# State-space pairs at other blocks, GELU and GLU three blocks on, half blocks of projection weights, and another order at the last gate

## The chip, the cores and the metric

One core of a Trainium2 chip (trn2) runs one program. The metric is the device time of one execution in microseconds (us), median of several runs. Five engines work side by side and meet only at semaphores: TensorE (PE, matmuls), VectorE (DVE), ScalarE (ACT), GpSimd (POOL) and SyncE (SP), which here issues the DMAs. Each engine works off its own list strictly in order.

## The reference

Two layers on x of shape (1, 256, 1024), all in float32. Cut to what matters here:

```python
def hybrid_layer(x, ...):
    h = x + 0.5 * swiglu(rms_norm(x, ffn1_norm), ffn1_w_in, ffn1_w_out)
    proj = rms_norm(h, mix_norm) @ w_in
    (sb_qkv, s5_u, gq, gk, gv, gr, gg, dsa_qkv, gates) = split(proj)
    y_sb = stick_breaking_attention(sb_q, sb_k, sb_v)
    y_s5 = s5_mixer(s5_u, ...)       # 1024 complex states, scan over time,
                                     # gelu(y) @ w_glu, then ga * sigmoid(gb)
    y_gla = gla_mixer(gq, gk, gv, gr, gg, ...)
    y_dsa = dilated_mixer(d_q, d_k, d_v, ...)
    gate = sigmoid(gates.reshape(bsz, seq, 4, 1024))
    per_branch = einsum('bsnw,nwd->bsnd', stack(y_sb, y_s5, y_gla, y_dsa), w_branch)
    h = h + sum(gate * per_branch, axis=2) @ w_out
    return h + 0.5 * swiglu(rms_norm(h, ffn2_norm), ffn2_w_in, ffn2_w_out)
```

## The kernel before

All weights come as one stream of blocks of 128 x 2048 floats (1 MB), into a ring of three slots (`raw`). SyncE issues the load of a slot when its last low part is written. A float32 weight is used as two fp32r parts: ScalarE rounds each half of a block (`round_half`, L802, L812) to `w_hi`, VectorE subtracts (`half_rest`, L1068, L1072) to get `w_lo`, and TensorE makes three matmuls of each product (L456 to L458): hi x hi, hi x lo, lo x hi. The activations are split in the same way (`split_pair`; L824 and L1084). So each block costs TensorE 48 matmuls of 256 columns, ScalarE two instructions and VectorE two.

A layer is: ffn 0 (33 blocks), mixer (31 blocks of `SEQ`, then 5 blocks of the output projection in `OUT_TILES`), ffn 1 (33 blocks). The change is in the mixer alone. For each block m, TensorE runs the block's product into bank 0 or 1 and then `pieces(m)` (L662), the small matmuls of the four branches; ScalarE rounds the block three ahead and then does its own `pieces(m)` (L948); VectorE evacuates bank m (L1478), makes the low part of the block three ahead, and does its `pieces(m)` (L1310). The order of each engine is thus written out by hand. Eleven of the blocks 0 to 12 are projections for the branches (`s5u` at 0 to `gr` at 12, dilated v at 11, linear v at 9); gates (q, n) fill blocks 7, 10, 13 to 23, 25, 27 and 29; `out0` to `out3` (blocks 24, 26, 28, 30) multiply the four branch outputs with w_branch.

State-space branch (S5), in four pairs of state tiles: `s5_in(pair)` on TensorE at block S5_AT[pair] into banks 6 and 7, `s5_rotate(pair)` (VectorE, L1252, waits for GpSimd's state of the pair before), one block later `s5_scan(pair)` (L1269, L1274), then GpSimd `s5_pair(pair)` (L1621, L1628 to L1634 and L1536), and four blocks after the rotation `s5_out(pair)` on TensorE (L600). After the last pair come the GELU (VectorE L1391 to L1402 at block 15, tanh on ScalarE, VectorE L1407 at 16), the GLU (TensorE at block 17, L707), tanh of the gate (ScalarE L1006), the product (VectorE L1417 at 18), and the split of the branch output (ScalarE L929, VectorE L1280).

Dilated attention: rotary product on VectorE at blocks 13 and 14 (ends with L1385), transposes by TensorE at 15 (L698), scores at 16 and 17, softmax and exponentials (L1286 to L1289, L997, L998) there, `dilated_weights` (L1292, L1295 to L1301) at 18 and 19, `dsa_turn` (L651, L658) at 19 and 20, the product with v at 21. Gated linear attention uses ScalarE at 16 for a logarithm and an exponential (L1002, L1003).

Banks 4 to 7 are shared: `gla_scores` (block 12) needs them after the last rotation.

After an out block, VectorE multiplies with the gates (`gate(dt)`, L1441, L1452), GpSimd adds the branches (`mix(dt)`, L1636), ScalarE and VectorE split the sum (`mixed_hi`, L1021 and L1025; `mixed_lo`, L1457 and L1459), and TensorE uses it in the output projection (`out_part`, L764). Two of the five projection blocks hold one tile of 128 columns only; their second half is zero and used by no matmul. After each, VectorE adds to h (L1509) and h is split for ffn 1.

Of the kernel before, what the change touches and what calls it, by code (L numbers as in the profile page):

```python
# [8 lines left out]
F32 = mybir.dt.float32  # L9
# [57 lines left out]
S5_AT = (1, 4, 7, 10)  # L67

LAST_OF_U = (3, 3)
MIXED_AT = [((0,), (1,)), ((), ()), ((), ()), ((2, 3, 4, 5, 6), (7,))]  # L70
# [155 lines left out]
def build(nc, x_in, stream, params_in, const_in, out):  # L226
    ctx = ExitStack()
    with ctx:
# [221 lines left out]
        def _(pe):  # L450
# [20 lines left out]
            for layer in range(LAYERS):  # L471
# [97 lines left out]
                def mixer():  # L569
# [16 lines left out]
                    def s5_in(pair):  # L586

                        if pair == 0:
                            pe.wait_ge(s.evac_v, layer * PER.evac_v + NTH[SLOT["s5u"]])
                        else:  # L590
                            pe.wait_ge(s.s5_rot, layer * PER.s5_rot + pair)
                        for part in range(2):
# [34 lines left out]
                    def gla_scores():  # L627
# [3 lines left out]
                        pe.wait_ge(s.s5_rot, layer * PER.s5_rot + ST // 2)  # L631
# [30 lines left out]
                    def pieces(m):  # L662
# [27 lines left out]
                        if m == 15:  # L690
# [3 lines left out]
                            pe.wait_ge(s.dsa_rope, layer * PER.dsa_rope + 1)  # L694
                            for side in range(2):
# [9 lines left out]
                        if m == 17:  # L705
                            dsa_scores(2), dsa_scores(3)
                            pe.wait_ge(s.s5_gelu, layer * PER.s5_gelu + 1)  # L707
# [7 lines left out]
                        if m == 19:  # L715
                            dsa_turn(0), dsa_turn(1)
                        if m == 20:
                            dsa_turn(2), dsa_turn(3)
# [71 lines left out]

        def ffn_steps(f):
# [9 lines left out]
        def _(act):  # L801
            def round_half(layer, k, slot, half):  # L802
# [6 lines left out]
                elif first_block(layer, k, slot):  # L809
# [3 lines left out]
                    .then_inc(s.w_hi, 1)  # L813

            def round_weights(layer, k, slot):

                round_half(layer, k, slot, 0)
                round_half(layer, k, slot, 1)
# [25 lines left out]
            for layer in range(LAYERS):  # L844
# [103 lines left out]
                def pieces(m):  # L948
# [39 lines left out]
                    if m == 15:  # L988
# [3 lines left out]
                        act.wait_ge(s.s5_inner, layer * PER.s5_inner + 1)  # L992
                        act.activation(s5g[:, 1, :], s5g[:, 1, :], ACT.Tanh).then_inc(s.s5_tanh, 1)
# [10 lines left out]
                    if m == 17:  # L1004
                        act.wait_ge(s.s5_glu, layer * PER.s5_glu + 1)
                        act.activation(s5g[:, 1, :], banks[:, 5, :], ACT.Tanh, scale=0.25).then_inc(s.s5_sig, 1)  # L1006
                    if m == 18:
                        act.wait_ge(s.y, layer * PER.y + 1)
                        branch_hi(1, yb[:, 0, :, :].rearrange("p a t -> p (a t)"), 0.25)
                    if m in (19, 20):  # L1010
                        for h in (2 * m - 38, 2 * m - 37):
                            act.wait_ge(s.dsa_pt, layer * PER.dsa_pt + h + 1)
                            act.activation(attB[:, h, :], banks[:, 6 + h % 2, 0:ATT], ACT.Copy) \
                                .then_inc(s.dsa_pte, 1)
                    if m == 21:
                        act.wait_ge(s.y, layer * PER.y + 2)
                        branch_hi(2, yb[:, 1, :, :].rearrange("p a t -> p (a t)"), 0.5)
# [772 lines left out]
```

## Time and profile before

| | |
|---|---|
| median of 3 runs | 1288.61 us (1288.47 to 1292.49) |
| profiled execution | 1289.22 us, its span 1287.3 us |
| granted TensorE clock, mean | 0.992 |
| TensorE busy | 1245.8 us (97%) |
| VectorE busy | 895.5 us (70%) |
| ScalarE busy | 640.0 us (50%) |
| GpSimd busy | 327.4 us (25%) |
| mixer of layer 0, layer 1 | about 209 to 455 us, 844 to 1090 us |

The span runs from the first to the last instruction of the profiled execution. The busy time of TensorE is an upper bound of its work, since matmuls overlap; the gap between two starts is the measure. A wait is put down to the engine whose semaphore came last; "issue" is time in which nothing that the profile shows was waited for, and the program's order then says what it was.

### The profile page before, as it was taken

Reading aid. Unit: us, or ns where it says so; the run is one execution under the profiler, and the core shown is the slowest. Engines: PE = TensorE matmul, PEld = TensorE weight load, DVE = VectorE, ACT = ScalarE, POOL = GpSimd, SP = SyncE. Lnnn points to the kernel's source line nnn. Section 1 sums busy time; section 2 is a strip of 40 time slices with the busy share of each in tenths; the row PEclk is TensorE's granted clock in tenths of the full one; section 3 lists DMA queues with packets and bytes.
Section 4 is the critical chain, followed back from the end, with each engine's and each line's share of the span. In section 5 each row is a group of like instructions: output and inputs, shape, how many; then the busy total and the mean of one; then the engine's idle time right before and its main releaser. Section 6 shows DMA issues by size and latency. Waiting matters only on the chain.

```text
span 1287.3 us, 25597 instructions
## 1 busy us (share of the span) xinstructions
PE 1245.8 (97%) x10328; PEld 1222.4 (95%) x10328; DVE 895.5 (70%) x1172; ACT 640.0 (50%) x904; POOL 327.4 (25%) x462
## 2 busy tenths in 40 slices
PE   5999999999999999999999999999999999999998
PEld 5999999888999999999999999998889999999998
DVE  4766857877877676555676687687887786656554
ACT  5654545663544454444456445557625444534432
POOL 0388800364003300000005895005630041000000
PEclk9999999998999999999999999999999999999999
DMA  7555554542344365555545545544333454555541
GB/s 299 199 185 174 180 179 165 175 149 99 131 158 166 135 236 198 191 195 168 191 135 201 188 165 200 189 164 152 135 130 131 154 186 160 201 184 175 186 173 66
DMA packets 31029, 220.46 MB, mean 171 GB/s; under 512 B 3568, under 2 KB 3568, under 8 KB 4592
## 3 DMA queue, kind: packets, MB, share of 16 engines
q1 hardware_dynamic: 30960, 219.49, 49.0%
q8 instruction: 50, 0.82, 0.3%
q14 instruction: 19, 0.16, 0.0%
HBM read 218.42 MB, written 1.05 MB: 170 GB/s over the span
## 4 chain that ended last, share of the span: by engine, by line
PE 75%; DVE 12%; POOL 7%; ACT 3%; issue 2%; DMA 0%; DVEq 0%; SPq 0%; ACTq 0%
PE banks L456 24%; PE banks L457 24%; PE banks L458 24%; DVE w_lo_t L1072 5%; PE banks L469 3%; ACT w_hi_t L812 1%; POOL st L1631 1%; DVE s5x L1274 1%; POOL s5x L1629 1%; POOL s5x L1628 1%; POOL st L1634 1%; POOL st L1536 1%; POOL st L1632 1%; DVE u_lo_t L1084 1%; DVE hT L1223 1%
## 5 line engine op out<-in xcount | busy, mean ns | idle before, releaser
L1072 DVE TENSOR_TENSOR w_lo_t<-raw,w_hi_t 128x1024 fp32r<-128x1024 f32 x408 | 518.0, 1310 | 107.8 <-ACT w_hi_t L812 107.4
L812 ACT ACTIVATE w_hi_t<-raw 128x1024 fp32r<-128x1024 f32 x408 | 407.2, 1046 | 126.7 <-PE banks L458 126.0
L456 PE MATMUL banks<-u_hi_t,w_hi_t 128*128 128x256 f32 x1520 | 436.0, 287 | 18.2 <-DVE w_lo_t L1072 14.1
L457 PE MATMUL banks<-u_lo_t,w_hi_t 128*128 128x256 f32 x1520 | 431.9, 284 | 0.0
L458 PE MATMUL banks<-u_hi_t,w_lo_t 128*128 128x256 f32 x1520 | 431.9, 284 | 0.0
L456 PEld LDWEIGHTS banks<-u_hi_t,w_hi_t 128*128 128x128 f32 x1520 | 293.6, 193 | 22.5 <-DVE w_lo_t L1072 14.1
L457 PEld LDWEIGHTS banks<-u_lo_t,w_hi_t 128*128 128x128 f32 x1520 | 293.8, 193 | 0.1
L458 PEld LDWEIGHTS banks<-u_hi_t,w_lo_t 128*128 128x128 f32 x1520 | 293.5, 193 | 0.0
L456 PE MATMUL banks<-b_hi_t,w_hi_t 128*128 128x256 f32 x864 | 245.1, 284 | 1.9 <-DVE b_lo_t L1084 1.9
L457 PE MATMUL banks<-b_lo_t,w_hi_t 128*128 128x256 f32 x864 | 244.5, 283 | 0.0
L458 PE MATMUL banks<-b_hi_t,w_lo_t 128*128 128x256 f32 x864 | 244.5, 283 | 0.0
L456 PE MATMUL banks<-h_hi_t,w_hi_t 128*128 128x256 f32 x672 | 190.9, 284 | 2.2 <-DVE h_lo_t L1177 1.2
L457 PE MATMUL banks<-h_lo_t,w_hi_t 128*128 128x256 f32 x672 | 190.4, 283 | 0.0
L458 PE MATMUL banks<-h_hi_t,w_lo_t 128*128 128x256 f32 x672 | 190.4, 283 | 0.0
L849 ACT ACTIVATE sbqk<-sbqk 128x256 f32<-128x256 f32 x88 | 36.8, 418 | 266.5 <-DVE sbqk L1167 266.5
L456 PEld LDWEIGHTS banks<-b_hi_t,w_hi_t 128*128 128x128 f32 x864 | 165.8, 192 | 2.3 <-DVE b_lo_t L1084 2.3
L457 PEld LDWEIGHTS banks<-b_lo_t,w_hi_t 128*128 128x128 f32 x864 | 165.8, 192 | 0.0
L458 PEld LDWEIGHTS banks<-b_hi_t,w_lo_t 128*128 128x128 f32 x864 | 165.8, 192 | 0.0
L456 PEld LDWEIGHTS banks<-h_hi_t,w_hi_t 128*128 128x128 f32 x672 | 129.3, 192 | 2.8 <-issue 1.3
L457 PEld LDWEIGHTS banks<-h_lo_t,w_hi_t 128*128 128x128 f32 x672 | 129.2, 192 | 0.0
L458 PEld LDWEIGHTS banks<-h_hi_t,w_lo_t 128*128 128x128 f32 x672 | 129.2, 192 | 0.0
L1167 DVE TENSOR_TENSOR sbqk<-banks,rstd_row 128x512 f32<-128x512 f32 x88 | 60.6, 689 | 74.5 <-PE banks L458 74.2
(215 smaller groups left out, 1267.7 us busy)
## 6 DMA issues: line engine op xcount, KB each, us to landing
raw<-weights SPq DMA_DIRECT2D x203, 1024.0 KB, 4.9
prm<-params SPq DMA_DIRECT2D x1, 1178.5 KB, 5.3
prm<-params SPq DMA_DIRECT2D x1, 1166.5 KB, 15.1
cst<-constants SPq DMA_DIRECT2D x1, 1027.0 KB, 11.1
hT<-x_t SPq DMA_DIRECT2D x2, 512.0 KB, 5.5
raw<-weights SPq DMA_DIRECT2D x2, 512.0 KB, 6.4
out_t<-hT SPq DMA_DIRECT2D x4, 256.0 KB, 2.2
prm<-params SPq DMA_DIRECT2D x1, 12.0 KB, 1.9
```

The costliest lines, as they stand in the source:

```text
L456: pe.matmul(o, st[0], mv[0], start=start, stop=False, skip_group_check=True)
L457: pe.matmul(o, st[0], mv[1], start=False, stop=False, skip_group_check=True)
L458: ins = pe.matmul(o, st[1], mv[0], start=False, stop=stop, skip_group_check=True)
L469: return pe.matmul(o, st, mv, start=start, stop=stop, skip_group_check=True)
L812: act.activation(w_hi[:, slot, a:a + HALF], raw[:, slot, a:a + HALF], ACT.Copy) \
L849: act.activation(ab[:, buf, 0, :], ab[:, buf, 0, :], ACT.Silu).then_inc(s.h_silu, 1)
L1072: dve.tensor_tensor(w_lo[:, slot, a:a + HALF], raw[:, slot, a:a + HALF], w_hi[:, slot, a:a + HALF].bitcast(F32), ALU.subtract).then_inc(s. ...
L1084: ins = dve.scalar_tensor_tensor(out=in_lo[where][:, kt, :], in0=hT[:, kt, :], scalar=p_(name)[:, kt:kt + 1], in1=in_hi[where][:, kt, :].b ...
L1167: dve.tensor_tensor(ab[:, buf, :, :], banks[:, bank, :].rearrange("p (c t) -> p c t", c=2), rstd_row[:, :].unsqueeze(1).to_broadcast([P, 2 ...
L1223: dve.scalar_tensor_tensor(out=hT[:, 2 * q:2 * q + 2, :].rearrange("p a t -> p (a t)"), in0=banks[:, q, :], scalar=0.5, in1=hT[:, 2 * q:2 ...
L1274: ins = dve.tensor_tensor_scan(s5x[:, i % 2, 1, part, :], decay, s5x[:, i % 2, 0, part, :], 0.0, ALU.mult, ALU.add)
L1536: own.link(pool.tensor_tensor(o, a, b, op))
```

## The change

Three edits, all in the mixer. (1) `S5_AT` becomes 1, 5, 9, 13, so the rotations, scans and outputs of pairs 1 to 3 move. `gla_scores` then stands before pair 3's product: it waits for three rotations instead of four, `s5_in(3)` waits for the masks of the linear attention, and the transposes at block 15 wait for the fourth rotation. The GELU moves from blocks 15 and 16 to 18 and 19, the GLU from 17 to 20, the gate's tanh to 20 and the product to 21, so that branch 2's split comes before branch 1's. (2) A one-tile block is rounded and subtracted in its first half only, and the semaphores count two for it; the splits of h for ffn 1 come after the weights. (3) At `out3`, VectorE does gate 6 before the four low parts, and gate 7 before the weights; ScalarE does `mixed_hi(6)` after the weights.

```diff
--- before.py
+++ after.py
...
 SS_AFTER, ROW_AFTER = 3, 5
-S5_AT = (1, 4, 7, 10)
+S5_AT = (1, 5, 9, 13)
 
 LAST_OF_U = (3, 3)
-MIXED_AT = [((0,), (1,)), ((), ()), ((), ()), ((2, 3, 4, 5, 6), (7,))]
+MIXED_AT = [((0,), (1,)), ((), ()), ((), ()), ((2, 3, 4, 5), (6, 7))]
 
...
                             pe.wait_ge(s.s5_rot, layer * PER.s5_rot + pair)
+                        if pair == 3:
+                            pe.wait_ge(s.gla_attm, layer * PER.gla_attm + HEADS)
                         for part in range(2):
...
                         pe.wait_ge(s.sb_exp, layer * PER.sb_exp + HEADS)
-                        pe.wait_ge(s.s5_rot, layer * PER.s5_rot + ST // 2)
+                        pe.wait_ge(s.s5_rot, layer * PER.s5_rot + 3)
                         for i in range(NGC):
...
                             pe.wait_ge(s.dsa_rope, layer * PER.dsa_rope + 1)
+                            pe.wait_ge(s.s5_rot, layer * PER.s5_rot + ST // 2)
                             for side in range(2):
...
                             dsa_scores(2), dsa_scores(3)
+                        if m == 19:
+                            dsa_turn(0), dsa_turn(1)
+                        if m == 20:
+                            dsa_turn(2), dsa_turn(3)
                             pe.wait_ge(s.s5_gelu, layer * PER.s5_gelu + 1)
...
                             ins.then_inc(s.s5_glu, 1)
-                        if m == 19:
-                            dsa_turn(0), dsa_turn(1)
-                        if m == 20:
-                            dsa_turn(2), dsa_turn(3)
                         if m == 21:
...
 
+        def one_tile(k, slot):
+
+            o = k * RING + slot - FFN_BLOCKS - NSEQ if isinstance(k, int) else -1
+            return 0 <= o < len(OUT_TILES) and len(OUT_TILES[o]) == 1
+
         def ffn_steps(f):
...
                 act.activation(w_hi[:, slot, a:a + HALF], raw[:, slot, a:a + HALF], ACT.Copy) \
-                    .then_inc(s.w_hi, 1)
+                    .then_inc(s.w_hi, 2 if one_tile(k, slot) else 1)
 
...
                 round_half(layer, k, slot, 0)
-                round_half(layer, k, slot, 1)
+                if not one_tile(k, slot):
+                    round_half(layer, k, slot, 1)
 
...
                         act.activation(dkT, banks[:, 7, :], ACT.Copy).then_inc(s.dsa_qk, 1)
-                        act.wait_ge(s.s5_inner, layer * PER.s5_inner + 1)
-                        act.activation(s5g[:, 1, :], s5g[:, 1, :], ACT.Tanh).then_inc(s.s5_tanh, 1)
                     if m in (16, 17):
...
                         act.activation(gn[:, 3, :], gn[:, 3, :], ACT.Exp, scale=-0.5).then_inc(s.gla_y0, 1)
-                    if m == 17:
-                        act.wait_ge(s.s5_glu, layer * PER.s5_glu + 1)
-                        act.activation(s5g[:, 1, :], banks[:, 5, :], ACT.Tanh, scale=0.25).then_inc(s.s5_sig, 1)
                     if m == 18:
-                        act.wait_ge(s.y, layer * PER.y + 1)
-                        branch_hi(1, yb[:, 0, :, :].rearrange("p a t -> p (a t)"), 0.25)
+                        act.wait_ge(s.s5_inner, layer * PER.s5_inner + 1)
+                        act.activation(s5g[:, 1, :], s5g[:, 1, :], ACT.Tanh).then_inc(s.s5_tanh, 1)
                     if m in (19, 20):
...
                                 .then_inc(s.dsa_pte, 1)
+                    if m == 20:
+                        act.wait_ge(s.s5_glu, layer * PER.s5_glu + 1)
+                        act.activation(s5g[:, 1, :], banks[:, 5, :], ACT.Tanh, scale=0.25).then_inc(s.s5_sig, 1)
                     if m == 21:
+                        act.wait_ge(s.y, layer * PER.y + 1)
+                        branch_hi(2, yb[:, 1, :, :].rearrange("p a t -> p (a t)"), 0.5)
                         act.wait_ge(s.y, layer * PER.y + 2)
-                        branch_hi(2, yb[:, 1, :, :].rearrange("p a t -> p (a t)"), 0.5)
+                        branch_hi(1, yb[:, 0, :, :].rearrange("p a t -> p (a t)"), 0.25)
                         act.wait_ge(s.dsa_o, layer * PER.dsa_o + 1)
...
                 dve.tensor_tensor(w_lo[:, slot, a:a + HALF], raw[:, slot, a:a + HALF],
-                                  w_hi[:, slot, a:a + HALF].bitcast(F32), ALU.subtract).then_inc(s.w_lo, 1)
+                                  w_hi[:, slot, a:a + HALF].bitcast(F32), ALU.subtract) \
+                    .then_inc(s.w_lo, 2 if one_tile(k, slot) else 1)
 
...
                 half_rest(layer, k, slot, 0)
-                half_rest(layer, k, slot, 1)
+                if not one_tile(k, slot):
+                    half_rest(layer, k, slot, 1)
 
...
 
+                    if m in (16, 17):
+                        dilated_softmax(2 * m - 32), dilated_softmax(2 * m - 31)
+                    if m == 16:
+                        dve.wait_ge(s.gla_tanh, layer * PER.gla_tanh + 1)
+                        own.link(dve.scalar_tensor_tensor(out=gn[:, 2, :], in0=gn[:, 2, :], scalar=1.0,
+                                                          in1=gr[:, :, :].rearrange("p a t -> p (a t)"),
+                                                          op0=ALU.add, op1=ALU.mult))
+                    if m == 18:
                         dve.wait_ge(s.s5_y, layer * PER.s5_y + ST // 2)
...
                             .then_inc(s.s5_inner, 1)
-                    if m in (16, 17):
-                        dilated_softmax(2 * m - 32), dilated_softmax(2 * m - 31)
-                    if m == 16:
+                    if m == 19:
                         dve.wait_ge(s.s5_tanh, layer * PER.s5_tanh + 1)
...
                                                  op0=ALU.add, op1=ALU.mult).then_inc(s.s5_gelu, 1)
-                        dve.wait_ge(s.gla_tanh, layer * PER.gla_tanh + 1)
-                        own.link(dve.scalar_tensor_tensor(out=gn[:, 2, :], in0=gn[:, 2, :], scalar=1.0,
-                                                          in1=gr[:, :, :].rearrange("p a t -> p (a t)"),
-                                                          op0=ALU.add, op1=ALU.mult))
                     if m in (18, 19):
                         dilated_weights(2 * m - 36), dilated_weights(2 * m - 35)
-                    if m == 18:
+                    if m == 21:
                         dve.wait_ge(s.s5_sig, layer * PER.s5_sig + 1)
...
                                                  op0=ALU.add, op1=ALU.mult).then_inc(s.y, 1)
-                    if m == 19:
-                        branch_lo(1, 1, yb[:, 0, :, :].rearrange("p a t -> p (a t)"), 0.25)
                     if m == 20:
...
                     if m == 22:
-                        branch_lo(2, 2, yb[:, 1, :, :].rearrange("p a t -> p (a t)"), 0.5)
+                        branch_lo(2, 1, yb[:, 1, :, :].rearrange("p a t -> p (a t)"), 0.5)
+                        branch_lo(1, 2, yb[:, 0, :, :].rearrange("p a t -> p (a t)"), 0.25)
                         branch_lo(3, 3, banks[:, 3, :], 1.0)
...
                             q = int(SEQ[m][3])
+                            gate(2 * q)
                             if q == 3:
...
                                     mixed_lo(dt)
-                            gate(2 * q)
+                                gate(2 * q + 1)
                             rest_of_weights(layer, k0 + m // RING + 1, m % RING)
-                            gate(2 * q + 1)
+                            if q < 3:
+                                gate(2 * q + 1)
                             continue
...
                             dve.wait_ge(s.res, layer * PER.res + 8 + q + 1)
-                        if o < 2:
-                            split_pair(layer * 3 + 2, "g_ffn2", q, where=1)
                         if o < 4:
                             rest_of_weights(layer, k0 + m // RING + 1, m % RING)
-                        if o in (2, 4):
+                        if o != 3:
                             split_pair(layer * 3 + 2, "g_ffn2", q, where=1)
```

## Rows read from the trace of the kernel before

**Rows 1.** The page, its first part: busy time of TensorE.

```profile
PE 1245.8 (97%) x10328; PEld 1222.4 (95%) x10328; DVE 895.5 (70%) x1172; ACT 640.0 (50%) x904; POOL 327.4 (25%) x462
```

**Rows 2.** Waits of TensorE over the whole span: us in total, times, longest.

```profile
PE banks L456 <- DVE w_lo_t L1072: 15.0, 2, 14.1
PE banks L469 <- POOL st L1634: 7.8, 6, 2.4
PE banks L469 <- issue: 5.6, 7, 2.2
PE banks L456 <- DVE u_lo_t L1459: 3.8, 2, 1.9
...
PE banks L456 <- DVE b_lo_t L1084: 1.9, 2, 1.0
```

**Rows 3.** Windows behind gaps: length, busy PE, PEld, DVE, ACT, POOL, clock, DMA.

```profile
248.50:260.50 12.00, 12.00 (x100) 11.39 (x101) 11.86 (x17) 5.68 (x10) 1.78 (x1) 1.00 0.26 90
...
884.10:898.10 14.00, 14.00 (x104) 13.37 (x104) 13.72 (x18) 6.19 (x12) 3.78 (x3) 0.88 0.21 76
304.20:319.20 15.00, 14.95 (x162) 14.33 (x163) 7.81 (x11) 0.60 (x1) 10.44 (x12) 0.66 0.42 141
939.60:951.50 11.90, 11.81 (x161) 11.07 (x162) 7.84 (x11) 0.60 (x1) 9.25 (x11) 0.86 0.50 178
...
1075.40:1087.60 12.20, 12.20 (x89) 12.20 (x90) 7.88 (x11) 8.66 (x12) 0.00 (x0) 0.86 0.25 88
```

**Rows 4.** Timeline of VectorE, blocks 4 to 11: start, duration, idle before it.

```profile
248.48 1.23 DVE L1262 TENSOR_TENSOR s5x<-banks,G 128x1024 f32<-128x1024 f32 x1 [4.40 <-POOL st L1634]
...
297.26 1.22 DVE L1262 TENSOR_TENSOR s5x<-banks,G 128x1024 f32<-128x1024 f32 x1
...
300.86 2.35 DVE L1072 TENSOR_TENSOR w_lo_t<-raw,w_hi_t 128x1024 fp32r<-128x1024 f32 x2
303.13 1.02 DVE L1322 SCALAR_TENSOR_TENSOR attA<-attA,cst 128x384 f32<-128x384 f32 x2
```

**Rows 5.** Timeline of GpSimd, its first, second and last step of pair 2.

```profile
281.69 0.74 POOL L1628 TENSOR_TENSOR s5x<-s5x,G 128x256 f32<-128x256 f32 x1 [9.42 <-DVE s5x L1274]
282.39 1.72 POOL L1629 TENSOR_TENSOR s5x<-s5x,G 128x256 f32<-128x256 f32 x1
...
293.41 1.59 POOL L1634 TENSOR_TENSOR st<-s5x,st 128x256 f32<-128x256 f32 x1
```

**Rows 6.** Timeline of VectorE from the end of block 13 to block 18.

```profile
319.27 0.69 DVE L1478 SCALAR_TENSOR_TENSOR G<-banks,rstd_row 128x512 f32<-128x512 f32 x1 [5.48 <-PE banks L458]
...
332.39 1.23 DVE L1385 TENSOR_TENSOR dqk<-dqk,G 128x1024 f32<-128x1024 f32 x1
...
337.49 0.86 DVE L1393 SCALAR_TENSOR_TENSOR s5x<-s5u,prm,banks 128x256 f32<-128x256 f32 x2
...
339.58 0.69 DVE L1401 TENSOR_TENSOR s5x<-s5x 128x512 f32<-128x512 f32 x1
...
352.50 2.36 DVE L1072 TENSOR_TENSOR w_lo_t<-raw,w_hi_t 128x1024 fp32r<-128x1024 f32 x2 [3.78 <-ACT w_hi_t L812]
...
361.80 0.29 DVE L1295 CUSTOM_DVE_ANT_0 attB<-attB,cst 128x128 f32<-128x128 f32 x1
```

**Rows 7.** Timeline of TensorE at blocks 15, 17, 18 and 19.

```profile
334.12 1.03 PE L698 MATMUL banks<-cst,dqk 128*128 128x128 f32 x8
...
348.50 3.72 PE L469 MATMUL banks<-s5x,prm 128*128 128x256 f32 x16
351.87 0.47 PE L456 MATMUL banks<-u_hi_t,w_hi_t 128*128 128x256 f32 x1
...
363.56 0.49 PE L658 MATMUL banks<-cst,attB 128*128 128x128 f32 x3
364.62 0.55 PE L658 MATMUL banks<-cst,attB 128*128 128x128 f32 x3 [0.57 <-DVE attB L1301]
```

**Rows 8.** Timeline of ScalarE at out3: the high part of tile 6.

```profile
434.89 0.42 ACT L1025 ACTIVATE u_hi_t<-U 128x256 fp32r<-128x256 f32 x1 [5.07 <-POOL U L1641]
```

## The prediction

> **What bounds the kernel now.** The page comes first: TensorE is busy for 97% of the span, so a change can only win TensorE's idle time or its slow clock, and can only lose by adding either [rows 1]. The waits of TensorE come second, since they say where the idle time is. One wait of 14.1 us is the start and is not touched. The rest is small and lies in the mixer of both layers: 7.8 us on GpSimd's state (L1634, six waits of s5_out), "issue" with 2.2 us in each layer (the first attention at block 12), 0.57 us on the dilated weights of block 19 and about as much at block 20 (L1301 [rows 7]), and at the end of the mixer 3.8 us on L1459, 1.9 us on L1084 and 0.9 us on L1072 [rows 2]. Third, the windows behind such gaps, for the granted clock. Seven gaps of 1.9 to 2.4 us stand in the mixers. Behind four the clock was partly 1.2 instead of 2.4 GHz: (1 - 0.88) x 14.0 = 1.7 us lost, (1 - 0.66) x 15.0 = 5.1 behind block 12 of layer 0, where the same work took 15.0 us against 11.9 in layer 1, 1.7 there, and 1.7 near the end; behind the other three, as at 248.5, it stayed at 2.4 [rows 3]. Last, the timelines of VectorE and GpSimd: the reader is to see there that VectorE's queue stands still before a rotation (4.40 us), and is late for the attention afterwards (L1322 starts at 303.13, and TensorE waits for it) [rows 4].
>
> I count in blocks m as the program does, 5.8 us each: two of them take from 351.87 to 363.56 [rows 7].
>
> **Part 1, early half (blocks 1 to 12).** Pair 1 to 3 move from blocks 4, 7, 10 to 5, 9, 13, and their outputs from 8, 11, 14 to 9, 13, 17. Pair 0 stays, and so does its wait at block 5 (2.0 us); s5_in(1) now fills time in front of it, and s5_rotate(1) no longer finds an unfinished state: the 4.40 us of idle VectorE go [rows 4]. Layer 0, in times of the old trace: rotation 1 now ends near 255.6, its scan near 264.0, behind block 6's weights and the softplus pieces. GpSimd needs 13.3 us for a pair (281.69 to 295.0); its steps take 0.74 alone and 1.7 beside L1072 [rows 5]. State 1 is there at 277.2. TensorE reaches s5_out(1) at 276.9 (block 9's end at 275.7, then s5_in(2)): a wait of 0.3 instead of 2.4. Then VectorE is what counts up to the attention. ScalarE ends its softplus part at 275.7, has rounded half of block 9 at 277.6, and from there VectorE has weights 2.3, masks 2.1, sum 1.4, rotation 3.6 (297.26 to 300.86 [rows 4]), evacuation 0.6, weights 2.3, gate products 2.9, scan 2.4, weights 2.9 beside GpSimd, L1322 1.0: 299.1. TensorE is ready at 297.6. So the attention starts 5.1 us earlier, but 2.1 us of that is work only put off (s5_in(3), s5_out(2)): a gain of **3.0 us**. In layer 1 the gap at block 5 was followed by the slow clock, and the wait at block 8 was 0.7, not 2.4: the slow clock hid in the wait. The gain is **1.4 us**. Bounds: 1.5 and 0.5 if GpSimd and VectorE block each other for one or two steps more; 4.6 and 2.9 if every wait behind block 5 goes. I take the middle, by the rows' durations.
>
> **Part 1, late half (blocks 13 to 23).** Here the moved work lands on VectorE in front of what TensorE needs. I count from the end of block 13, which is 319.2 in the old trace [rows 6].
> - Block 15: the transposes (L698) need the rotary product L1385, which ends at 333.5, +14.4, with TensorE there at +14.9 (334.12 [rows 7]). Rotation 3 (3.6 us) now stands before it in block 13: +18.0. TensorE has s5_in(3) and s5_out(2) more and the old s5_out(3) less: +16.1. A new wait of **2.0 us**. The added wait for s5_rot is met long before.
> - Block 17: scan 3 ends at +20.4, and GpSimd needs 12.7 to 13.5 us beside two blocks of weights (8.8 if nothing blocks it): +33.2 to +33.9. TensorE is at s5_out(3) at +31.7. A wait of 2 us, which the next step would contain anyway.
> - Block 19: the head weights of the dilated attention. The chain is block 16's end (+24.9), weights, softmax of heads 0 and 1 (+31.3), ScalarE's exponentials and the two table loads (4.7), weights of block 17 from +37.0 (old row: VectorE idle 3.78 for ScalarE), softmax of heads 2 and 3 (+41.6), weights of block 18 (+43.5 to +45.8). Now the GELU, 2.8 us (337.49 to 340.27), stands before the head weights, 2.7 us (361.80 to 364.5) [rows 6]: +51.2. In the old order the GLU's 3.4 us on TensorE (348.50 to 351.87) were the cover for this chain: its wait was only 0.57 [rows 7]. The GLU is now at block 20, so TensorE finishes block 19 at +47.1 and waits 4 us. Block 20 starts at +51.6; in the old order it started at +45.7 with the GLU done. Without GLU and with the two moved pieces it should have been +44.5: lost **7.1 us**, the 2.0 of block 15 among them.
> - Block 20: the wait on L1301 there goes with its restart, since VectorE is ahead by then: 0.9 back. The GLU costs the same 3.4 there. Block 21 to out0: s5's output, three L1280 instead of two behind block 22's weights end at +79.7, out0 is reached at +80.2. Nothing lost, with 0.5 us to spare.
> Together **+6.1 us** per layer. Bounds: 4 (if the weights find ScalarE earlier) and 9 (if GpSimd lengthens the weights of blocks 15 and 16 and the 0.5 us of spare is used up).
>
> **Part 2 and 3, the end of the mixer.** Old: ScalarE waits 5.07 us for GpSimd's mix before it rounds out3's successor [rows 8], VectorE's weights come after that, then gate 7, then mix 7, and TensorE waits 1.9. Now gate 6 starts at 430.1, gate 7 ends at 433.8, mix 7 on GpSimd at 437.8 at worst, and its low part is there at 438.7, for a need at 440.9. The four L1459 pushed behind gate 6 end from 431.7 to 432.7, one after the other, and TensorE first needs one at 433.0. The halved blocks take 2 x 1.0 us from ScalarE and 2 x 1.2 us from VectorE per layer, and the splits go behind the weights. Block 34 is then ready 5 us early, and the last split ends at 458.1 for a need at 459.0. All of these waits should go: 3.8 + 1.9 + 0.9 = 6.6 us, with restarts of 0.1 to 0.3 us each and 0.3 at the sum of squares 7.6, and 1.5 us of slow clock in layer 1 (of the 1.7, the part in which TensorE has work) [rows 2, 3]: **-9.1 us** for both layers (4.5 + 4.6). Bounds: -9.5 and -6, where the last split comes late by its margin of 0.9 and the slow clock comes anyway. The DMA queue only profits: it waits for the same counter, which now jumps by two.
>
> **The clock.** The new waits at blocks 15 and 19 come in both layers. Four of seven gaps were followed by 1.2 GHz [rows 3], at about 1.6 us: 4 x 0.57 x 1.6 = **+3.6 us**, from 0 to 6.4. The slow clock behind block 17's wait would be hidden in block 19's. The Trainium skill (TensorE: Matmul & The Clock Gate, "Why this matters for your kernels") has the throughput drop only after idle gaps longer than those here; by that these 3.6 us would be nothing. This trace does not agree: gaps of about 2 us were followed by the drop.
>
> **The sum.** -3.0 - 1.4 + 6.1 + 6.1 - 9.1 = -1.3 us, and with the clock +2.3 us. The profiled execution took 1289.2 (span 1287.3 and 1.9 around it), the median is 1288.6, 0.6 lower: 1291.5 for a profile, 1290.9 for the median.
>
> **Rivals.**
> A, no difference to be measured (within 0.3%, 3.9 us, which is about what this kernel's measurement can tell from none): the mid-mixer loses what the end wins. My forecast, 1290.9, alone 1286 to 1293. Chance 0.47.
> B, slower: the dilated chain at block 19 is the one mechanism. For it speaks that everything from block 16 on is one chain through VectorE and ScalarE without slack. It decides from 7.5 us per layer on, or from the slow clock behind all four waits: +2.8 + 2.8 on top of the sum: 1293 to 1298, about 1295.5. Chance 0.34.
> C, faster: the 4.40 us that VectorE no longer idles are carried to block 13, or ScalarE lets the weights of blocks 17 and 18 through earlier, so that block 19 waits 2 us less, and the clock holds: -1.3 - 4 = -5.3 and less, about 1283. Against it: VectorE already has 5.48 us idle before 319.27, so a lead ends there [rows 6]. By the skill's rule on the clock alone the sum would be 1287.3, still A. Chance 0.17.
> D, the end does not do what it says (the low parts stay late, as gate 7 and the weights collide with GpSimd): 9.1 becomes 4: 1296, which is B's side. Chance 0.02.
>
> Faster 0.17, same 0.47, slower 0.36. The range goes from 1284.0, into C, to 1298.0, the end of B.
>
> **What would show it.** Right: waits of TensorE on L1634 at block 8 gone, a wait before L698 of 2 us, a wait before L658 at block 19 of 3 to 5 us with the GELU rows directly before the L1295 rows, and L1459 gone from the waits. Wrong: L658 waits below 2 us, or the attention at block 12 waiting over 3 us.

## The result, and the profile after

The changed kernel takes 1282.8 us (median of 6 runs, 1282.3 to 1286.0) against 1288.6; the ratio is 0.995, with a 95% interval of 0.9935 to 0.9966. It is 0.5% faster. The forecast was 1290.9 with a range down to 1284.0: wrong in sign and 1.2 us outside. The profiled execution has a span of 1281.1 us, 6.2 less than before.

The page of the changed kernel, first part [rows 1]:

```profile
PE 1243.2 (97%) x10328; PEld 1220.3 (95%) x10328; DVE 899.9 (70%) x1168; ACT 636.3 (50%) x900; POOL 335.7 (26%) x462
```

Its waits of TensorE over the span (total, times, longest), to be read beside [rows 2]:

```profile
PE banks L456 <- DVE w_lo_t L1081: 14.3, 1, 14.3
PE banks L469 <- POOL st L1646: 8.6, 6, 2.0
PE banks L660 <- DVE attB L1312: 6.2, 4, 2.7
PE banks L701 <- DVE dqk L1396: 3.4, 2, 1.7
PE banks L456 <- DVE h_lo_t L1188: 1.2, 1, 1.2
PE banks L469 <- issue: 0.6, 3, 0.2
```

Before, the head weights had this line, which [rows 2] leaves out:

```profile
PE banks L658 <- DVE attB L1301: 2.5, 4, 0.7
```

The reader is to see that the waits of the mixer's end are gone (L1459, L1084 and the second of L1072; 6.6 us), that "issue" fell by 5.0, that a new wait stands before the transposes at block 15 (3.4), and that the one for the head weights at block 19 grew (6.2 instead of 2.5). In all the waits fell by little, from 38.0 to 34.5 us. The sum by stretch, both layers together (from the timelines; 2.05 us of work per layer is only put off from the first stretch to the third):

| stretch | forecast | measured |
|---|---|---|
| s5_out(0) to the attention at block 12 | -5.1 - 3.4 | -6.5 - 6.4 |
| from there to the end of block 13 | 0 | -3.2 - 0.1 |
| end of block 13 to out0 | +8.15 + 8.15 + 3.6 (clock) | +11.2 + 9.2 |
| out0 to the sum of squares for ffn 1 | -9.1 | -5.2 - 5.2 |
| sum | +2.3 | -6.2 |

The timeline of TensorE (start, duration, idle before it): s5_out(0), s5_out(1), the transposes, s5_out(3), and the two turns of block 19. The attention of block 12, at 298.24, has no wait.

```profile
248.94 1.06 PE L469 MATMUL banks<-st,s5c 128*32 128x256 f32 x8 [1.36 <-POOL st L1646]
...
278.04 1.06 PE L469 MATMUL banks<-st,s5c 128*32 128x256 f32 x8 [0.95 <-POOL st L1646]
...
298.24 1.57 PE L469 MATMUL banks<-attA,sbv 128*64 128x256 f32 x16
...
328.08 1.09 PE L701 MATMUL banks<-cst,dqk 128*128 128x128 f32 x8 [1.70 <-DVE dqk L1396]
...
343.69 1.06 PE L469 MATMUL banks<-st,s5c 128*32 128x256 f32 x8 [1.96 <-POOL st L1646]
...
360.05 0.55 PE L660 MATMUL banks<-cst,attB 128*128 128x128 f32 x3 [2.74 <-DVE attB L1312]
361.39 0.90 PE L660 MATMUL banks<-cst,attB 128*128 128x128 f32 x3 [0.79 <-DVE attB L1312]
```

VectorE in front of block 19, from the weights of block 18's turn to the head weights; the four lines L1412 to L1420 are the GELU, 355.88 to 358.65:

```profile
353.60 2.36 DVE L1081 TENSOR_TENSOR w_lo_t<-raw,w_hi_t 128x1024 fp32r<-128x1024 f32 x2 [1.22 <-ACT w_hi_t L820]
355.88 0.87 DVE L1412 SCALAR_TENSOR_TENSOR s5x<-s5u,prm,banks 128x256 f32<-128x256 f32 x2
...
357.96 0.69 DVE L1420 TENSOR_TENSOR s5x<-s5x 128x512 f32<-128x512 f32 x1
358.57 0.28 DVE L1306 CUSTOM_DVE_ANT_0 attB<-attB,cst 128x128 f32<-128x128 f32 x1
...
360.98 0.35 DVE L1312 TENSOR_SCALAR attB<-attB,dmx 128x256 f32<-128x256 f32 x1
```

Windows behind waits (length, busy PE, PEld, DVE, ACT, POOL, clock, DMA), beside [rows 3]: 12 us from the attention of block 12 in layer 0 and in layer 1, and block 20 of layer 0.

```profile
298.20:310.20 12.00, 12.00 (x163) 11.45 (x164) 6.00 (x8) 2.52 (x4) 10.08 (x12) 0.86 0.49 176
929.60:941.60 12.00, 12.00 (x163) 11.47 (x164) 6.03 (x8) 2.56 (x4) 10.06 (x12) 0.86 0.51 176
...
361.90:370.10 8.20, 8.20 (x50) 8.20 (x49) 5.44 (x18) 1.39 (x3) 0.00 (x0) 0.66 0.38 130
```

### The profile page after: what moved, and what is told of

Same layout as the page of the kernel before. It is cut to its first block, busy times and chain, and to the rows that moved or that the text cites. A ratio compares the mean times of both kernels' runs of the same rounds, so it can differ in the third digit from the quotient of the medians.

```text
span 1281.1 us, 25591 instructions
## 1 busy us (share of the span) xinstructions
PE 1243.2 (97%) x10328; PEld 1220.3 (95%) x10328; DVE 899.9 (70%) x1168; ACT 636.3 (50%) x900; POOL 335.7 (26%) x462
## 4 chain that ended last, share of the span: by engine, by line
PE 84%; DVE 8%; POOL 5%; ACT 2%; issue 1%; DMA 0%; SPq 0%; DVEq 0%; ACTq 0%
PE banks L456 27%; PE banks L458 27%; PE banks L457 27%; PE banks L469 3%; DVE w_lo_t L1081 3%; POOL st L1643 1%; POOL s5x L1641 1%; DVE s5x L1285 1%; ACT w_hi_t L820 1%; POOL st L1646 1%; POOL s5x L1640 1%; POOL st L1644 1%; DVE u_lo_t L1095 1%; POOL st L1548 1%; DVE hT L1234 1%
## 6 DMA issues: line engine op xcount, KB each, us to landing
cst<-constants SPq DMA_DIRECT2D x1, 1027.0 KB, 11.2
```

## The experiments

All are timed in three rounds against the kernel before on the same chip (its median there 1289.6 to 1290.0). My theory once the result was known: the end wins about 10 us; the late half loses what was forecast; the forecast was wrong about the early half, where it had counted on a wait at block 12 and left the slow clock behind it as it was, and neither came so. The rival: the late half cost less than forecast, and the end did not bring what it should.

### The end alone, and the pairs alone

The first kernel has parts 2 and 3 of the diff, with the pairs, GELU and GLU of before (against the changed kernel, cut to its first lines):

```diff
-S5_AT = (1, 5, 9, 13)
+S5_AT = (1, 4, 7, 10)
...
```

> The kernel before with parts 2 and 3 only (half blocks for the one-tile projection blocks, splits behind the weights, gates 6 and 7 ahead of the weights at out3). Theory: the whole gain of the change comes from here. From out0 to the sum of squares the kernel before takes 74.4 us in each layer and the changed one 69.1; so this kernel is 10.5 us faster than before (about 1278), and L1459, L1084 and L1072 are gone from TensorE's waits but for the start. Rival: the late low parts are late because of the order in blocks 13 to 23; then a part of the 5.2 us per layer stays and the gain is 7 us or less.

Measured: 1276.9 us (1275.1 to 1277.1), ratio 0.990 (0.988 to 0.991): 12.8 faster. Its waits of TensorE:

```profile
PE banks L469 <- POOL st L1642: 7.5, 5, 2.4
PE banks L469 <- issue: 4.3, 5, 2.2
PE banks L658 <- DVE attB L1309: 2.5, 4, 0.7
```

The second has part 1 alone:

> The changed kernel with parts 2 and 3 undone: only the pairs, the GELU and the GLU are moved. Theory: this part alone loses. Early half -6.5 and -6.4 us up to the attention of block 12 (2.1 of each only put off), -3.1 less slow clock behind it, late half +11.2 and +9.2: together +4.3, about 1293; waits before L698, s5_out(3) and the dilated turns as in the changed kernel. Rival: the move wins by itself (removed GpSimd waits), then it is below 1287.

Measured: 1294.8 us (1292.3 to 1297.3), ratio 1.004 (1.002 to 1.006): 5.2 slower. Its waits hold both new ones at the sizes of the changed kernel, and those of the end are back. The late half cost no less than forecast: from the attention of block 14 to the sum of squares it took 9.2 and 9.8 us more than before, 19.0 together, where the forecast's terms for this part make 17.8. With the end's gain that puts the rival out. Its waits:

```profile
PE banks L660 <- DVE attB L1310: 6.2, 4, 2.8
PE banks L456 <- DVE u_lo_t L1469: 3.7, 2, 1.9
PE banks L701 <- DVE dqk L1394: 3.4, 2, 1.7
```

So the pairs lose and the end wins, as forecast, but by +5.2 instead of +11.4 (-3.0 - 1.4 + 12.2 + 3.6), and by -12.8 instead of -9.1. The stretch from the first turn of block 19 to the sum of squares fell by 5.2 us per layer in the end-only kernel too, 10.5 together. The rest of its 12.8 is not in the end: from the attention of block 12 to that of block 14, where nothing was edited, its profiled execution took 18.5 and 17.0 us against 21.7 and 18.6 before, behind waits of 1.5 and 2.2 against 2.2 and 2.2. The clock over the first 12 us was 0.86 and 1.00 there, 0.57 and 0.86 before. Since the edit stands behind this stretch in each layer, no run shows that it has a part in that.

### Is the wait at block 12 a matter of chance?

The changed kernel once more, with nothing edited:

> The changed kernel once more, for the scatter of its wait at block 12. In e_norm12 the VectorE rows of layer 0 are the changed kernel's to 0.05 us up to 294.77, then two L1081 take 2.88 instead of 2.34 us and two L1333 2.09 instead of 1.02, and TensorE waits 1.5 us at the attention. Theory: at that point GpSimd's first step of pair 2 and VectorE's weights start within some hundredths of a microsecond, and which is first decides; so the same kernel shows the wait in some executions and not in others: total 1282 to 1286, TensorE's issue wait of 1.5 us zero, one or two times in the profile. Rival: the wait belongs to what e_norm12 changed; then it is absent here.

Measured: 1283.1 us (1281.6 to 1285.1). In layer 0 the attention of block 12 now waits 1.50 us, in layer 1 not at all. VectorE of this run and its attention on TensorE, then VectorE of the changed kernel's first profile: the weights and the masks L1333, for which the attention waits.

```profile
294.00 2.88 DVE L1081 TENSOR_TENSOR w_lo_t<-raw,w_hi_t 128x1024 fp32r<-128x1024 f32 x2
296.80 2.09 DVE L1333 SCALAR_TENSOR_TENSOR attA<-attA,cst 128x384 f32<-128x384 f32 x2
```

```profile
298.98 1.54 PE L469 MATMUL banks<-attA,sbv 128*64 128x256 f32 x16 [1.50 <-issue]
```

```profile
294.81 2.34 DVE L1081 TENSOR_TENSOR w_lo_t<-raw,w_hi_t 128x1024 fp32r<-128x1024 f32 x2
297.06 1.02 DVE L1333 SCALAR_TENSOR_TENSOR attA<-attA,cst 128x384 f32<-128x384 f32 x2
```

GpSimd in the same two, its first step of pair 2:

```profile
294.16 1.63 POOL L1640 TENSOR_TENSOR s5x<-s5x,G 128x256 f32<-128x256 f32 x1 [17.00 <-DVE s5x L1285]
```

```profile
294.97 3.70 POOL L1640 TENSOR_TENSOR s5x<-s5x,G 128x256 f32<-128x256 f32 x1 [16.99 <-DVE s5x L1285]
```

Both start 0.16 us behind VectorE's weights. In one execution GpSimd's step ends in 1.63 us and VectorE's two steps take 2.88 + 2.09; in the other VectorE's run through in 2.34 + 1.02 and GpSimd stands for 3.70. Six of the profiles have this order up to here, two layers each: in eight of the twelve starts GpSimd stood for 3.7 to 3.9 us, in four it took 1.6. The 1.6 us that VectorE gains or loses are the wait at block 12. The Trainium skill (SBUF — State Buffer, "Who interferes with whom") says that which of the two engines is held up depends on the order in which their instructions are issued; these rows agree that they hold up each other, and show that with the same order, 0.16 us apart, either can be the one. I had forecast 2.9 and 1.0, which lies between the two cases, and took it for certain. Yet the wait alone does not decide the time: the profiled execution with it took 1281.6 us, the one without it 1283.0, since the clock over the 12 us behind the attention was 1.00 in both layers of the first and 0.86 in both of the second.

### Does the slow clock behind block 12 come from the wait?

Two additions of 128x1024 are put in front of the masks of block 11 (their result isn't read):

```diff
...
+                    if m == 11:
+                        for n in range(2):
+                            own.link(dve.tensor_tensor(yb[:, :, :, :].rearrange("p a b t -> p (a b) t"),
+                                                       hT[:, 0:4, :], hT[:, 4:8, :], ALU.add))
                     if m in (8, 11):
```

> The changed kernel with two additional VectorE operations of 1.2 us (sums into a tile that is free there) in front of the last two masks at block 11, so that TensorE waits some 2.2 us at the attention of block 12, as in the kernel before. Theory: the 10.2 us of slow clock behind block 12 in layer 0 of the kernel before need this wait in front of the small matmuls; with it back, the stretch from the attention to the end of block 13 grows from 11.9 towards 15 us in at least one layer, and the kernel loses 4.4 us for the waits and up to 6 for the clock: 1287 to 1293. Rival: the slow clock comes from the 96 matmuls of 32 x 32 alone (behind which the changed kernel shows 3.4 us of it without any wait); then the stretch stays at 11.9 us and the loss is 4.4 us or less, since VectorE and TensorE waits later absorb a part.

Measured: 1303.3 us (1299.3 to 1304.4), ratio 1.010: 20 us above the changed kernel, and 10 above the band of the theory. The rival, in which the stretch behind the attention stays at 11.9 us, did not hold either. Its additions and the masks behind them, its attention at block 12 in layer 0, and the 12 us behind it:

```profile
297.04 2.88 DVE L1332 TENSOR_TENSOR yb<-hT 128x1024 f32<-128x1024 f32 x2
299.96 1.97 DVE L1337 SCALAR_TENSOR_TENSOR attA<-attA,cst 128x384 f32<-128x384 f32 x2
```

```profile
302.02 2.17 PE L469 MATMUL banks<-attA,sbv 128*64 128x256 f32 x16 [3.75 <-issue]
```

```profile
302.00:314.00 12.00, 11.97 (x137) 11.37 (x138) 5.28 (x7) 0.60 (x1) 7.94 (x9) 0.57 0.25 89
```

The wait is 3.75 us where I expected 2.2: the additions took 2.88 us instead of 2.4, and the masks, which now met GpSimd's steps, 1.97 instead of 1.02. Both layers together waited 7.5 us, and from the attention of block 12 to that of block 14 they took 22.9 us each instead of 19.8. In the profiled execution, the fastest of the four and 16.3 us longer than the changed kernel's, that makes 6.9 us in each layer, 3.7 of wait and 3.2 of clock. Most of the rest lies at places where nothing was edited: in layer 0 1.9 us came back in the late half, where block 20 had the full clock, in layer 1 1.9 were lost there, and 1.7 by the clock behind block 5, ahead of the edit and behind the same wait of 1.36 us. That last stretch, in this run and in the changed kernel:

```profile
885.70:899.70 14.00, 13.98 (x104) 13.20 (x105) 11.09 (x16) 5.77 (x12) 0.00 (x0) 0.88 0.25 78
```

```profile
880.30:894.30 14.00, 13.98 (x113) 13.27 (x114) 12.55 (x19) 7.27 (x17) 0.00 (x0) 1.00 0.32 109
```

The other three executions are 3.2 to 5.1 us longer, with a mean clock of 0.981 to 0.984 against 0.986, and have no profile.

The clock over the 12 us behind the attention, in the 24 layers of all twelve profiles, by the wait in front of it: 0 to 0.3 us, 1.00 in ten and 0.86 in four; 1.5 us, 1.00 in four and 0.86 in one; 2.2 us, 0.57, 0.86 and 1.00; 3.7 us, 0.57 in both. So 0.57 was seen behind waits of 2.2 us and more only, and 0.86 behind none, 1.5 and 2.2; what else decides is not settled. For the forecast it means that of the 5.1 us lost in layer 0 of before [rows 3] a part could go with its 2.2 us wait, and I had left them where they were.

### The new waits of the late half

The head weights in front of the GELU pieces at blocks 18 and 19:

> The changed kernel with one swap on VectorE: at block 18 the head weights of heads 0 and 1 stand ahead of the GELU, and at block 19 those of heads 2 and 3 behind the GELU's last step as before. Theory: the 2.7 us of the GELU in front of the head weights are the wait at block 19: it falls from 3.5 us to 0.8 to 1.3, but ScalarE's tanh waits 2.7 us longer for the GELU in front of its rounding of block 19, so the weights of block 19 and the head weights 2 and 3 are late, and some 3 us of wait come up at block 20: 0 to 2 us faster than the changed kernel. Rival: the wait at 19 is only order, nothing comes up at 20, and the kernel is 5 to 7 us faster (1276 to 1278).

Measured: 1285.2 us (1282.2 to 1286.3), 2.4 above the changed kernel where 0 to 2 below it were expected; the ranges overlap. The edit puts the head weights first at block 19 too, which the expectation has otherwise. Its turns at blocks 19 and 20 in layer 0, and the GLU of layer 1:

```profile
357.45 0.55 PE L660 MATMUL banks<-cst,attB 128*128 128x128 f32 x3 [0.20 <-DVE attB L1312]
365.50 0.55 PE L660 MATMUL banks<-cst,attB 128*128 128x128 f32 x3 [1.76 <-DVE attB L1312]
366.84 0.90 PE L660 MATMUL banks<-cst,attB 128*128 128x128 f32 x3 [0.79 <-DVE attB L1312]
...
999.79 6.27 PE L469 MATMUL banks<-s5x,prm 128*128 128x256 f32 x16
```

The wait of 2.74 at block 19 fell to 0.20 and stands at block 20 instead, so the GELU was what delayed the head weights, and VectorE is late anyhow. The GLU, now right behind that wait, took 5.0 and 6.3 us in the two layers instead of 3.6; the clock was 0.86 and 0.72 over the 12 us from the waiting turn.

Next, the dilated norm and gain moved from block 13 to block 12, so that they don't stand in front of rotation 3:

```diff
-                    if m == 13:
-                        branch_lo(0, 0, banks[:, 2, :], 1.0)
                         dve.wait_ge(s.dsa_y0, layer * PER.dsa_y0 + 1)
                         newton(dms[:, 1, :], dms[:, 2, :], dms[:, 3, :], dms[:, 4, :])
...
                         own.wait(n)
+                    if m == 13:
+                        branch_lo(0, 0, banks[:, 2, :], 1.0)
```

> The changed kernel with the norm and gain of the dilated q and k (3.4 us of VectorE, which stood in front of the last rotation at block 13) moved to block 12, behind the masks, where VectorE idles 5.4 us. Theory: the wait before the transposes of block 15 (1.7 us) is VectorE's order; it goes, and since the scan, GpSimd's last pair, and the softmax chain come earlier too, the wait for the last pair at block 17 (2.0) falls below 0.5. But the weights of block 17 hang on ScalarE, so block 19 keeps its wait: 3 to 4 us faster than the changed kernel for both layers, about 1279. Rival: the freed time is given back in block 19 entirely, 0 to 1 us faster; second rival: the slow clock decides, and the times scatter by 3 us whatever the waits.

Measured: 1279.5 us (1277.7 to 1279.9), 3.3 less than the changed kernel. The wait before the transposes is gone; of the 1.7 us per layer that it had, 0.7 came back before the head weights of layer 0 (3.44 instead of 2.74). The wait for the last pair at block 17, expected below 0.5, was 1.36.

Third, that, with besides the last masks at block 10 instead of 11, the head weights first, and the GELU at 19, its last step at 20 and the GLU at 21 (each one block later):

> e_norm12 with the last two masks (L1333) at block 10 instead of 11, the GELU at block 19 behind all head weights, its tanh and last step at 20, and the GLU at 21. Theory: VectorE has 2.9, 2.2 and 3.3 us idle behind blocks 19 to 21 of the changed kernel, enough for the GELU; the wait at block 19 falls below 1 us and none takes its place, the two windows of slow clock of 6.8 us behind it go too, and the wait at block 12 can't come up: 1264 to 1270. Rival: the branch's output is now late for out0 (three splits behind block 22's weights had 0.5 us of spare by my sum); then TensorE waits on L1291 before out0 for 1 to 4 us and the kernel stays above 1272.

Measured: 1270.1 us (1268.6 to 1271.5), ratio 0.985 (0.983 to 0.987), 13 us less than the changed kernel and 7 less than the end alone. Its waits, 25 us of layer 0 behind the attention of block 12, and 10 us of block 20:

```profile
PE banks L469 <- POOL st L1645: 8.2, 7, 1.4
PE banks L660 <- DVE attB L1311: 3.1, 4, 0.8
```

```profile
301.00:326.00 25.00, 24.58 (x224) 22.34 (x221) 24.69 (x34) 8.66 (x11) 7.98 (x8) 1.00 0.40 138
...
355.60:365.60 10.00, 10.00 (x87) 10.00 (x86) 9.76 (x25) 5.10 (x9) 0.00 (x0) 1.00 0.41 149
```

In the first VectorE (third of the busy times) is full, 24.69 of 25.00 us. The second shows what the wait at block 19 costs besides its length. Over 10 us, from 1.9 us behind the start of the first turn that waits, the clock was 1.00 in all ten layers of the profiles where that wait is 0.8 us or less, 0.84 to 1.00 in the six where it is 1.9 to 2.0, and 0.72 to 0.82 in the six where it is 2.7 to 3.4 (left out is the first kernel of this section, whose long wait lies inside the 10 us). Four of the profiles have both waits in one program: 1.9 us in one layer left 0.88 to 1.00, 2.7 us in the other 0.72 to 0.78. The long wait goes with the slow clock here.

### What is left: the waits for GpSimd

On top of the last kernel, the outputs of the pairs go to blocks 6, 10, 13 and 18 instead of 5, 9, 13 and 17:

> e_cover with the outputs of the pairs (s5_out) at blocks 6, 10, 13 and 18 instead of 5, 9, 13 and 17. Theory: TensorE's waits on GpSimd (1.4, 1.0 and 1.4 to 2.0 us per layer) are nothing but the block at which the output is asked for; all go, 4 us per layer at most minus nothing: 7 to 8 us faster than e_cover, 1257 to 1262. Rival: GpSimd waits for the output of the pair before it overwrites its state, so that its next pair comes later and the wait moves to the later pairs; then less than 4 us.

Measured: 1268.8 us (1266.8 to 1269.6). 7 to 8 us less were expected, 1257 to 1262; 1.3 came. That is in the rival's band, but its mechanism isn't there: each first step of GpSimd is released by VectorE's scan. The waits:

```profile
PE banks L661 <- DVE attB L1312: 5.2, 4, 2.0
PE banks L470 <- POOL st L1646: 1.2, 1, 1.2
```

Seven us of waits for GpSimd went, two of waits for VectorE came, and the time stayed. The same with the last output back at block 17:

> e_out_later, with one change: the output of the last state-space pair is back at block 17, the other three stay at blocks 6, 10 and 13. It asks why moving the outputs later gave 1.3 us where 8 to 12 were expected. Theory P: the wait of TensorE for GpSimd at block 17 had been cover for the head weights, so that taking it away only moved it to block 19. Then, with the output back at 17, the wait there returns (1.4 us in each layer), the one for the head weights at block 19 falls by as much, and the time is that of e_out_later within 2 us, 1267 to 1270. Rival Q: the longer stretch at block 18 (the output and the dilated products behind each other) made the wait at block 19 by itself. Then the wait for the head weights falls from 2.0 to 0.8 us at most, the wait for GpSimd at block 17 stays under 0.5, and the time is 1263 to 1265.

Measured: 1266.5 us (1265.2 to 1269.1), ratio 0.981 (0.979 to 0.983); the wait at block 17 is back, 1.35 us in each layer. The longest, 3.42, is the one at block 13 of layer 1, in a profiled execution that is the slowest of the four. The waits, then these two outputs of layer 1:

```profile
PE banks L470 <- POOL st L1646: 7.2, 4, 3.4
PE banks L661 <- DVE attB L1312: 3.1, 4, 0.8
```

```profile
932.24 1.29 PE L470 MATMUL banks<-st,s5c 128*32 128x256 f32 x8 [3.42 <-POOL st L1646]
...
963.82 1.06 PE L470 MATMUL banks<-st,s5c 128*32 128x256 f32 x8 [1.35 <-POOL st L1646]
```

The time is 0.5 below the band of the one theory and 1.5 above that of the other, and the waits speak for the first: with the wait of 1.35 at 17 the longest for the head weights is 0.8 instead of 2.0, so the one was cover for the other. Counted from the mixer's first sum of squares in layer 0, TensorE comes to block 12 2.3 us earlier than with the outputs at 5 and 9 (80.3 against 82.7), but GpSimd's first step of pair 3 starts only 1.6 us earlier (109.8 against 111.4), behind a VectorE that was busy for 25.69 of the 26 us from 299 on. VectorE looks like the bound of this stretch; no run shortened its work there.

Last, the old places of the pairs, with the end's edits and the same two moves of VectorE's work (norm at 12, masks at 10):

> The edits to the projection blocks and the last gate alone (as in e_end_only), with the old places of the pairs (1, 4, 7, 10) and of GELU and GLU, and besides the masks of heads 2 and 3 one block earlier (block 10) and the dilated norm and gain at block 12. It asks whether the new spacing of the pairs is worth anything once VectorE's other work is moved out of blocks 11 and 13, as it was in e_cover (1270.1). Theory P: the spacing itself brings little, since what it gains at blocks 8 and 11 it gives back at 15 to 20; the old places with the same two moves come to 1268 to 1273. Rival Q: the spacing is needed, since the old places keep the wait for GpSimd at block 11 and VectorE is full at blocks 10 to 12, so that the two moves help little or nothing: 1274 to 1278, and the masks at block 10, behind the rotation, may even make the attention at block 12 wait.

Measured: 1275.6 us (1275.4 to 1276.2), ratio 0.989 (0.987 to 0.990).

```profile
PE banks L469 <- POOL st L1642: 12.3, 8, 2.4
PE banks L658 <- DVE attB L1309: 2.4, 4, 0.7
PE banks L469 <- DVE b_lo_t L1288: 1.4, 2, 0.7
```

The two moves take the wait at block 12 away and bring 1.3 us; 4.8 us more are spent on GpSimd's state. So the rival's band holds: the wider spacing, with the head weights ahead of the GELU and the GLU at block 21, is worth about 5.5 us (1275.6 against 1270.1). As the change made it, it cost 5.2. The attention at block 12 didn't wait for the masks, as the rival had thought it might.

## Why the prediction was wrong

- **What bounds the kernel**, held: gains and losses were TensorE's waits and its clock.
- **Early half, the wait at block 12.** This step failed. Its sum of VectorE's rows gave 299.1 for the end of L1322, 50.7 us behind s5_out(0), and with it a wait of 1.5 us in each layer. In the profile of the result the masks ended at 49.1, and there was no wait. Of the 1.6 us, 0.9 arose before the last weights, which started 45.9 us behind s5_out(0) instead of 46.8: above all, the gate products took 2.4 us and not the 2.9 of the old row, beside which GpSimd wrote a state [rows 5] while here it stood idle (the 16.99 above). The rest is 3.36 instead of 3.9 for the last weights and the masks. Run again, the kernel had the masks' end at 50.8; that this is the number of my sum is luck, since 0.9 too late a start and 1.1 too little for the collision cancel. The better case lay at my bounds (gains of 4.6 and 2.9; 4.5 and 4.3 were measured), and I took the middle for both. The wait of 0.3 us at block 9 was 0.95: TensorE was there 0.3 us earlier and the state 0.3 later than in my sum, with GpSimd's 13.3 us for the pair as forecast.
- **Early half, the clock.** This step failed too. I had put layer 1 at 1.4 us instead of 3.0 for a slow clock behind block 5. It didn't come in this execution, where the wait at block 5 was 1.36 us in both layers, against 2.01 in both before; behind the same 1.36 us it did come in layer 1 of two other runs whose kernels are the same up to there (0.88 over 14 us: the additions in front of block 12, and the head weights first), so this part of the gain is partly luck. The 5.1 us behind block 12 of layer 0 are priced at nothing in my sum, though I had listed them among the losses and had shortened the wait in front of them; 3.2 came back. These terms together are 7.7 of the 8.5 us that the sum was off. How much of the 7.7 belongs to the change and how much to the execution stays open.
- **Late half.** Right step by step: counted from the end of block 13 the transposes started at +18.0 (forecast +18.1), the output of pair 3 at +33.6 (33.6) with a wait of 1.96 (2), the weights of block 17 at +37.0 (37.0), the second softmax ended at +41.7 (41.6), the head weights at +51.2 (51.2), block 20 started at +51.8 (51.6). The stretch is 3.1 us over the steps in layer 0, where block 20 ran at 0.66, and 1.1 in layer 1, 4.1 in all, where I had 3.6 for the clock. In layer 1 the clock was 0.86 over the 12 us behind block 17's wait; I had taken that as hidden in the wait at block 19, but its first turn started 0.7 us later than in layer 0.
- **The end.** Forecast -9.1, measured -10.5; the bound of -9.5 was too tight by 1.0. In layer 0, with the full clock on both sides, 3.9 us of waits brought 5.2, so the restarts and the sum of squares gave 1.4 us instead of 0.7. All of these waits went.
- **The rivals.** C gave the time (about 1283) by luck, not by its cause: block 19 waited as forecast, and the gain came ahead of block 13. B's loss was nearly there (9.1 us in layer 0 and 7.1 in layer 1, the work put off taken out and the clock counted in) and was outweighed. D is refuted by the end alone.

## What to carry to other kernels

A wait on a path costs its length and perhaps a slow clock behind it; whoever takes such a wait away has to price the slow stretch behind it as a possible gain, not only price new waits as a possible loss, and has to take the clock from more than one execution. Where two engines start within 0.2 us of each other and block each other, keep both outcomes as cases with their own chance instead of the middle. And a wait that is removed in a full stretch has to be followed to the next one: here the head weights, the state of pair 3 and the transposes stood behind one VectorE without a pause, so only moving its work to where it had pauses (block 12 from 13, block 10 from 11, the GELU behind the head weights) made the time fall, to 1270.1 us, and to 1266.5 with the outputs of the first two pairs one block later.

## What the runs showed of the hardware

- The same program, executed twice, had VectorE's two steps at 3.36 and at 4.97 us and GpSimd's at 3.70 and 1.63, from a start with the same 0.16 us between them.
- Two additions of 2.9 us on VectorE in front of block 12 cost 20 us by the medians and 16.3 in the profiled executions, of which 7.5 are the waits and 6.3 the clock right behind them. The granted clock was 0.57 over 12 us behind a wait of 3.75 us, in which TensorE worked 11.97 of the 12.
- Behind no wait at all the clock was 0.86 in both layers in one execution and 1.00 in another (layer 1). What decides between these is open; no run here separates the small 32x32 products that follow the attention from the wait in front of it.
- Behind block 19, where no such small products follow, the clock went with the wait: 1.00 behind 0.8 us and less, 0.72 to 0.82 behind 2.7 us and more.
